# A decoder layer's first microseconds: all of x's copies on VectorE, both variances moved up, long constant products between the turns

## The chip, the cores and the metric

The kernel runs on one core of one Trainium2 chip. The metric is the device time of one execution in microseconds (us); the figure before is the median of three runs.

## The reference, cut to what matters

One decoder layer over 512 tokens with 16 learned meta tokens ahead of them (528 in all), model width 1024, all in float32:

```python
def rmsnorm(x, g):
    y = x32 * lax.rsqrt(jnp.mean(x32 * x32, axis=-1, keepdims=True) + EPS)
    return y * g

def swiglu(h, w_gate, w_up, w_down):
    return (jax.nn.silu(h @ w_gate) * (h @ w_up)) @ w_down

h = concatenate([meta, x])                                    # 528 x 1024
h = h + 0.5 * swiglu(rmsnorm(h, ffn1_norm), ffn1_w_gate, ffn1_w_up, ffn1_w_down)
h = h + token_mixing(rmsnorm(h, mix_norm), ...)               # linear and sparse attention
h = h + 0.5 * swiglu(rmsnorm(h, ffn2_norm), ...)
return rmsnorm(h, final_norm)[:, N_META:]
```

Only the first two lines of the layer matter here: how x gets into the kernel's layout, its first norm, and the first products of the first feed-forward part (FFN). The hidden width of that part is 2816.

## The kernel before

The kernel is one program per engine, each in an order written out by hand, with semaphores between them. The activations are kept turned: `h` is 128 features (partitions) by 8 feature tiles by 528 tokens. float32 products of weights are made of three products of two-part operands: a high part (`xh`, `wh`) and a rest (`xl`, `wl`). ScalarE makes the high parts of weights (`hi(u)` for unit u) and of x (`high_x`), GpSimd makes the rests of weights (`lo(u)`), VectorE the rests of x.

**The start**, which is what the change touches. SyncE issues the loads of x in four tiles of 128 tokens, then of the first four weight units; ScalarE's queue issues the 16 meta tokens and the vectors (gains, biases). Then:

- TensorE first runs ten products of the constants `ones` and `ident`, 128 columns each, into a bank that nobody reads (L2511). Then it turns x: ten *turns* n = 0 to 9, each four transposes of 128x128 (two turns per token tile; turns 0 and 1 are the meta tokens, 16 wide), turn n into PSUM bank n mod 8 (L2540), with one transpose of the vectors ahead of turn 4 (L2531).
- Each turn is copied from PSUM to `h` by `keep_x` (L448 to L456): turns 0 to 8 on VectorE (L456), turn 9 on ScalarE (L454).
- ScalarE squares and sums each 128-token tile of x straight from the loaded rows (L2049), VectorE that of the meta tokens (L2317). `x_variance(0)` (L2310, L2312; VectorE, after the copy of turn 5) is for the meta tokens and tiles 1 and 2, `x_variance(1)` (after the copy of turn 7) for tiles 3 and 4. `x_roots` (L2040, ScalarE) takes the root of each; the first one stands in ScalarE's order between the squares of tile 3 and of tile 4.
- The roots are put on diagonals: tiles 0 to 2 by GpSimd (L1835), tiles 3 and 4 by ScalarE (L2056). TensorE's `spread(0)` and `spread(1)` (L2522) multiply `ones` with them, which puts each token's factor on all partitions (PSUM banks 6 and 7). `spread(0)` waits for eight copies (`x_kept` 8).
- VectorE waits for all copies and for the spread, then makes `xn` = h times gain times factor, one of eight feature tiles at a time (L2336), then the eight rests `xl` (L2341), which need ScalarE's `xh` (L1912).
- ScalarE: diagonals, copy of turn 9, `hi(0)` (L1885), four `xh`, `hi(1)`, four `xh`, and on to `hi(2)`.
- TensorE's `first_products` (L2406) is six groups of 16 matmuls, 264 columns each: `wh`(unit 0) with `xh`, `wl`(0) with `xh`, `wh`(1) with `xh`, `wl`(1) with `xh`, then `wh`(0) and `wh`(1) with `xl`. Only the first group waits for each `xh`, and the fifth for each `xl`. After them comes the next unit's product (L2371), and from there to the end of the kernel TensorE is fed almost without a pause.

Of the kernel before, what the change touches and what calls it, by code (L numbers as in the profile page):

```python
# [26 lines left out]
ACT = mybir.ActivationFunctionType  # L27
AX_X = mybir.AxisListType.X

P = 128  # L30
# [179 lines left out]
def build(nc, x, meta, ffn1, ffn2, mix_norm, w_in, w_a2, b_a, head_norm, w_out, final_norm,  # L210
          cos_t, sin_t, out):
    ctx = ExitStack()
    with ctx:  # L213
        def sb(name, shape, dt=F32, scope=ctx):
            return scope.enter_context(nc.sbuf_tensor(name, shape, dt))

        def sem(name):
            return ctx.enter_context(nc.semaphore(name))

        ps = ctx.enter_context(nc.psum_tensor("ps", [P, 8, 512], F32))  # L220
# [14 lines left out]
        ident = sb("ident", [P, P])  # L235
        ones = sb("ones", [P, P])
# [140 lines left out]
        x_turned, x_kept = sem("x_turned"), sem("x_kept")  # L377
# [64 lines left out]
        def x_cols(n):  # L442


            t = n // 2
            return (META + (t - 1) * P, P) if t else (0, META)

        def keep_x(eng, n):  # L448
            c, w = x_cols(n)
            eng.wait_ge(x_turned, n + 1)  # L450
            src = ps[:, n % 8, 0:4 * w].rearrange("p (k n) -> p k n", k=4)
            dst = h[:, 4 * (n % 2):4 * (n % 2) + 4, c:c + w]
            if n == 9:
                eng.activation(dst, src, ACT.Copy).then_inc(x_kept_act, 1)  # L454
            else:
                eng.tensor_copy(dst, src).then_inc(x_kept, 1)  # L456

        x_kept_act, x_squared = sem("x_kept_act"), sem("x_squared")

        x_inv, x_root, x_spread = sem("x_inv"), sem("x_root"), sem("x_spread")  # L460
        x_diag, x_diag_pool = sem("x_diag"), sem("x_diag_pool")
# [4 lines left out]
        def x_pieces(t):  # L466

            c, w = x_cols(2 * t)
            return [(a, max(c, a * HALF) - a * HALF, slice(max(c, a * HALF) - c, min(c + w, (a + 1) * HALF) - c))
                    for a in range(2) if max(c, a * HALF) < min(c + w, (a + 1) * HALF)]  # L470
# [65 lines left out]
        def pe_mixer(pe, product, product_k, norm_product):  # L536
# [166 lines left out]
            def tails(e):  # L703

                b, _, s, w = att_step(0)
                if e == 0:
                    pe.wait_ge(v_kept, 6)
                else:
                    pe.wait_ge(tail_done, 1)
                for hd in range(e, HEADS, 2):  # L710
                    rows = slice(HD * e, HD * (e + 1))
                    mm = pe.matmul(ps[0:w, TAIL_BANK, tail_cols(hd)], pjb[rows, hd // 2, s:s + w],
                                   pjb[rows, 4 + hd // 2, 512:TOK], start=True, stop=True)
                mm.then_inc(tail_done, 1)
# [312 lines left out]
        def act_mixer(act, hi, prep_hi, root):  # L1027
            def keep_part(bank, dst, u, parts):
                ((_, t, n),) = parts
                act.wait_ge(w_used, Q_USED[u])  # L1030
                act.activation(dst[:, t:t + n], ps[:, bank, 0:n], ACT.Copy).then_inc(pj_kept, 1)
# [607 lines left out]
        def _(sp):  # L1639
# [24 lines left out]
            def ffn_loads(weights, u0, number):  # L1664
                _, w_gate, w_up, w_down = weights
                gate_v = w_gate.rearrange("(k p) f -> p k f", p=P)
                up_v = w_up.rearrange("(k p) f -> p k f", p=P)
                down_v = w_down.rearrange("(k p) d -> p k d", p=P)
                for f in range(PLAIN):
                    for e, v in enumerate((gate_v, up_v)):  # L1670
                        load(u0 + 2 * f + e, v[:, :, f * P:(f + 1) * P], cols())

                def load_down(g, d):
                    f0, cnt = GROUPS[g]
                    load(U_DOWN[number, g, d], down_v[:, f0:f0 + cnt, d * P:(d + 1) * P],
                         lambda s: s[:, 0:cnt * P].rearrange("p (k n) -> p k n", k=cnt))

                for d in range(PRE_DOWN):
                    load_down(0, d)
                for g, (f0, cnt) in enumerate(GROUPS):  # L1680
                    for m in range(cnt if g else 0):
                        for e in range(2):
                            f = f0 + 2 * (m // 2) + e
                            load(U_PAIR[number, g, m] + e, (up_v if m % 2 else gate_v)[:, :, f * P:(f + 1) * P], cols())
                        for e in range(2):
                            load_down(*step_down_of(g, m, e))
                for d in range(KT):
                    load_down(len(GROUPS) - 1, d)
# [188 lines left out]
        def _(act):  # L1877
            def hi(u):
                slot, n, c = u % RING, WIDTH[u], -(-WIDTH[u] // HALF_UNIT)
                if u == U_MIX + M_IKW:  # L1880
                    act.wait_ge(ikw_loaded, 16)
                act.wait_ge(w_in_slot[slot], 16 * (u // RING + 1))
                if Q_FREE[u]:
                    act.wait_ge(w_used, Q_FREE[u])
                act.activation(places(0, PLACE[u], c)[:, 0:n], raw[:, slot, 0:n], ACT.Copy).then_inc(w_hi, c)  # L1885
# [168 lines left out]
            act.wait_ge(x_root, 2)  # L2054
            for t in range(3, 5):
                act.activation(diag[:, t, :], ident[:, :], ACT.Copy, scale=xvar[:, t:t + 1]).then_inc(x_diag, 1)  # L2056
            keep_x(act, 9)
            hi(0)
            for d in range(KT):
                high_x(d)  # L2060
# [13 lines left out]
        def _(dve):  # L2074
# [233 lines left out]
            def x_variance(i):  # L2308
                dve.wait_ge(x_squared, X_PARTS[i].stop - 1)
                dve.tensor_scalar(xvar[:, X_PARTS[i]], xsum[:, X_PARTS[i]], 1.0 / D, EPS, ALU.mult, ALU.add).then_inc(x_inv, 1)  # L2310
                dve.wait_ge(x_inv, 2 * i + 2)
                dve.reciprocal(xvar[:, X_PARTS[i]], xvar[:, X_PARTS[i]]).then_inc(x_inv, 1)  # L2312
# [3 lines left out]
            meta_squares = t01[0:META, :, :].rearrange("p f n -> p (f n)")[:, 0:D]  # L2316
            dve.tensor_tensor_reduce(out=meta_squares, in0=xin[0:META, 0, :], in1=xin[0:META, 0, :], scale=1.0, scalar=0.0,  # L2317
                                     op0=ALU.mult, op1=ALU.add, accum_out=xsum[0:META, 0:1]).then_inc(x_inv, 1)
            for n in range(9):
                if n == 4:  # L2320
                    dve.wait_ge(vecs_turned, 1)
                    dve.tensor_copy(vecs[:, :], ps[:, 7, 0:4 * KT + 3]).then_inc(vecs_kept, 1)
                keep_x(dve, n)
                if n == 5:
                    dve.wait_ge(x_inv, 1)
                    x_variance(0)
                if n == 7:
                    x_variance(1)
            dve.wait_ge(x_kept, 9)
            dve.wait_ge(x_kept_act, 1)  # L2330
            dve.sem_inc(h_done, KT)
            dve.wait_ge(vecs_kept, 1)
            dve.wait_ge(x_spread, 5)
# [23 lines left out]
        def _(pe):  # L2357
# [149 lines left out]

            pe.wait_ge(consts, 2)

            for n in range(10):  # L2510
                pe.matmul(ps[:, 6, 0:P], ones[:, :], ident[:, :], start=True, stop=True)  # L2511

            def spread(i):

                for t in range(X_PARTS[i].start, X_PARTS[i].stop):
                    if i == 0:
                        pe.wait_ge(x_diag_pool, t + 1)
                    else:
                        pe.wait_ge(x_diag, t - X_PARTS[1].start + 1)
                    n = P if t else META  # L2520
                    for bank, c, cols in x_pieces(t):
                        mm = pe.matmul(ps[:, 6 + bank, c:c + cols.stop - cols.start], ones[0:n, :], diag[0:n, t, cols],  # L2522
                                       start=True, stop=True)
                    mm.then_inc(x_spread, 1)

            for n in range(10):
                t, half = n // 2, n % 2
                w = x_cols(n)[1]
                if n == 4:
                    pe.wait_ge(const_loaded, 96)  # L2530
                    pe.transpose(ps[:, 7, 0:4 * KT + 3], vec_rows[:, :],  # L2531
                                 ident[0:4 * KT + 3, 0:4 * KT + 3]).then_inc(vecs_turned, 1)
                if n == 7:
                    pe.wait_ge(vecs_kept, 1)
                pe.wait_ge(x_loaded[t], 16)
                if n >= 8:
                    pe.wait_ge(x_kept, n - 7)
                for k in range(4):
                    c = (4 * half + k) * P
                    mm = pe.transpose(ps[:, n % 8, k * w:(k + 1) * w], xin[0:w, t, c:c + P], ident[0:w, 0:w])  # L2540
                mm.then_inc(x_turned, 1)

            pe.wait_ge(x_kept, 8)
            spread(0)
            spread(1)
            ffn(U_FFN1, 0, 0)
            pe_mixer(pe, product, product_k, norm_product)
            ffn(U_FFN2, 1, 2)
# [2 lines left out]
            for n in range(8):  # L2551
                half, t = divmod(n, 4)
                tokens = slice(META + t * P, META + (t + 1) * P)
                if n == 4:
                    pe.wait_ge(ss_done, 4 * KT)
                    for c in range(4):
                        mm = pe.matmul(ps[:, 7, c:c + 1], ss[:, META + c * P:META + (c + 1) * P], ones[:, 0:1],  # L2557
                                       start=True, stop=True)
# [45 lines left out]
```

## Time and profile before

| | |
|---|---|
| median of three runs | 1070.98 us (1069.23 to 1072.9) |
| the profiled execution: its own time | 1073.09 us |
| its span | 1071.4 us |
| TensorE matmul busy | 1047.1 us (98%) |
| VectorE, ScalarE, GpSimd busy | 781.4, 464.2, 659.0 us |
| mean granted TensorE clock | 0.993 |

The profile is one execution. Its time and span differ by 1.7 us, which lies outside the instructions. In rows of the timeline the first figure is the start and the second the time from the first start to the last end of the merged instructions. PE is TensorE, DVE VectorE, ACT ScalarE, POOL GpSimd. The granted clock is recorded as a share of 2.4 GHz; ahead of its first recorded event, at 11 us, it is shown as 1.00, and there the durations must be read instead.

### The profile page before, as it was taken

What the parts mean: (1) busy time and instruction counts of PE and PEld (TensorE: products, weight loads), DVE (VectorE), ACT (ScalarE), POOL (GpSimd) and SP (SyncE); (2) the same over time, 40 slices, a digit from 0 to 9 for tenths busy, and PEclk for the clock granted to TensorE, in tenths of its full rate; (3) what the DMA queues carried; (4) which work ended last, traced back from release to release, by engine and by line L of the source; (5) the groups of instructions that cost most, each with busy time, mean ns of one, the idle gap of its engine ahead of it and who ended that gap; (6) DMA issues with size and microseconds to landing.
All of it is one profiled execution on the core that took longest, in us unless ns stands there. A gap on an engine that the chain in (4) does not pass through costs nothing. (4 is left out here: it accounts for less than half of the span.)

```text
span 1071.4 us, 19526 instructions
## 1 busy us (share of the span) xinstructions
PE 1047.1 (98%) x7427; PEld 946.1 (88%) x7427; DVE 781.4 (73%) x1251; ACT 464.2 (43%) x732; POOL 659.0 (62%) x747
## 2 busy tenths in 40 slices
PE   8999999999999999999999999999899999999997
PEld 7999999999999997788767678778799999999986
DVE  6647897677675587699575596478879977877835
ACT  6424444334343354552355526453434443443425
POOL 4948677787686277089721303356767877777840
PEclk8999999999999999999999999999999999999999
DMA  6233243323332344344321101222233434333321
GB/s 198 85 96 94 78 113 112 110 83 105 108 106 75 107 117 111 81 117 117 85 58 40 41 21 60 79 67 81 72 98 99 118 109 112 87 108 109 89 59 79
DMA packets 172256, 98.69 MB, mean 92 GB/s; under 512 B 6787, under 2 KB 167606, under 8 KB 172166
## 3 DMA queue, kind: packets, MB, share of 16 engines
q1 hardware_dynamic: 172064, 97.38, 32.3%
q8 instruction: 59, 0.97, 0.4%
q14 instruction: 31, 0.25, 0.1%
q10 hardware_dynamic: 102, 0.08, 0.0%
HBM read 91.18 MB, written 2.10 MB: 87 GB/s over the span
## 5 line engine op out<-in xcount | busy, mean ns | idle before, releaser
L1776 POOL TENSOR_TENSOR wl<-raw,wh 128x256 fp32r<-128x256 f32 x292 | 250.4, 892 | 212.6 <-ACT wh L1885 173.2
L1776 POOL TENSOR_TENSOR wxl<-raw,wxh 128x256 fp32r<-128x256 f32 x240 | 230.3, 985 | 151.6 <-ACT wxh L1885 151.2
L2371 PE MATMUL ps<-ah,wxh 128*128 128x264 f32 (+1 forms) x456 | 122.4, 323 | 2.8 <-DVE h L2175 2.4
L2371 PE MATMUL ps<-ah,wxl 128*128 128x264 f32 (+1 forms) x456 | 122.2, 322 | 0.0
L2371 PE MATMUL ps<-al,wxh 128*128 128x264 f32 (+1 forms) x456 | 122.0, 322 | 0.0
L2175 DVE SCALAR_TENSOR_TENSOR h<-ps,h 128x528 f32<-128x528 f32 (+1 forms) x96 | 66.5, 693 | 70.1 <-PE ps L2371 70.1
L2371 PE MATMUL ps<-xh,wh 128*128 128x264 f32 (+3 forms) x336 | 102.6, 348 | 2.3 <-DVE h L2175 1.1
L2490 PE MATMUL ps<-xh,wh 128*128 128x264 f32 (+1 forms) x360 | 102.1, 284 | 0.9 <-DVE h L2175 0.9
L2490 PE MATMUL ps<-xl,wh 128*128 128x264 f32 (+1 forms) x360 | 102.0, 283 | 0.0
L2490 PE MATMUL ps<-xh,wl 128*128 128x264 f32 (+1 forms) x360 | 101.6, 282 | 0.0
L2371 PE MATMUL ps<-xl,wh 128*128 128x264 f32 (+3 forms) x336 | 97.4, 332 | 0.0
L2371 PE MATMUL ps<-xh,wl 128*128 128x264 f32 (+3 forms) x336 | 97.2, 332 | 0.0
L1885 ACT ACTIVATE wxh<-raw 128x512 fp32r<-128x512 f32 (+2 forms) x88 | 53.3, 607 | 76.4 <-PE ps L2371 76.4
L2371 PEld LDWEIGHTS ps<-ah,wxh 128*128 128x128 f32 x456 | 75.7, 188 | 8.6 <-POOL wxl L1776 2.5
L2371 PEld LDWEIGHTS ps<-ah,wxl 128*128 128x128 f32 x456 | 75.9, 189 | 6.8
L2371 PEld LDWEIGHTS ps<-al,wxh 128*128 128x128 f32 x456 | 76.0, 189 | 5.2
L1776 POOL TENSOR_TENSOR wl<-ws,wh 128x256 fp32r<-128x256 f32 x72 | 69.0, 990 | 9.4 <-ACT wh L1903 9.4
L2371 PEld LDWEIGHTS ps<-xh,wh 128*128 128x128 f32 (+1 forms) x336 | 57.2, 187 | 18.7 <-issue 9.4
L1926 ACT ACTIVATE ah<-ubuf 128x528 fp32r<-128x528 f32 (+1 forms) x36 | 23.0, 640 | 110.7 <-DVE ubuf L2278 99.9
L2490 PEld LDWEIGHTS ps<-xh,wh 128*128 128x128 f32 x360 | 68.1, 189 | 1.6 <-DVE wl L2138 1.1
L2490 PEld LDWEIGHTS ps<-xl,wh 128*128 128x128 f32 x360 | 67.9, 189 | 0.5
L2490 PEld LDWEIGHTS ps<-xh,wl 128*128 128x128 f32 x360 | 68.0, 189 | 0.0
(319 smaller groups left out, 2975.0 us busy)
## 6 DMA issues: line engine op xcount, KB each, us to landing
raw<-in_ffn_w_gate SPq DMA_DIRECT2D x44, 512.0 KB, 4.1
raw<-in_ffn_w_up SPq DMA_DIRECT2D x44, 512.0 KB, 4.7
raw<-in_ffn_w_down SPq DMA_DIRECT2D x80, 256.0 KB, 2.8
raw<-in_w_in SPq DMA_DIRECT2D x28, 512.0 KB, 4.1
raw<-in_w_out SPq DMA_DIRECT2D x8, 512.0 KB, 3.4
xin<-in_x SPq DMA_DIRECT2D x4, 512.0 KB, 5.8
raw<-in_ffn_w_down SPq DMA_DIRECT2D x16, 128.0 KB, 2.2
out<-xin SPq DMA_DIRECT2D x4, 512.0 KB, 3.6
```

Of the source, the lines that this page charges most:

```text
L1776: op = pool.tensor_tensor(dst[:, part], src[:, part], high[:, part].bitcast(F32), ALU.subtract)
L1885: act.activation(places(0, PLACE[u], c)[:, 0:n], raw[:, slot, 0:n], ACT.Copy).then_inc(w_hi, c)
L1926: act.activation(ah[:, j, tk], src, ACT.Copy).then_inc(a_hi, 1)
L2175: dve.scalar_tensor_tensor(out=as_parts(h[:, d, tk], norm), in0=psum_parts(bank, norm), scalar=0.5, in1=as_parts(h[:, d, tk], norm), op0=A ...
L2371: mm = pe.matmul(ps[0:m, bank + a, 0:width], places(lo, PLACE[u], -(-WIDTH[u] // HALF_UNIT))[:, k * P:k * P + m], r[:, tile, t:t + width], ...
L2490: mm = pe.matmul(ps[:, seven_bank(v, i), 0:w], places(lo, at_p[wn], 1)[:, k * P:(k + 1) * P], x_operand(xlo, xn_, w, number)[:, k, :], sta ...
```

## The change

- `keep_x` of turn 9 moves from ScalarE to VectorE; its own semaphore `x_kept_act` goes, and VectorE waits for ten `x_kept`.
- `x_variance(0)` moves from after the copy of turn 5 to after that of turn 3, `x_variance(1)` from after turn 7's to after turn 6's.
- On TensorE the ten constant products of 128 columns become two of 512 columns, into bank 3. One more of these follows each of turns 5, 7 and 9, and one follows `spread(1)`. The one after turn 5 waits for the copy of turn 3, since it overwrites bank 3.

```diff
         def keep_x(eng, n):
...
-            if n == 9:
-                eng.activation(dst, src, ACT.Copy).then_inc(x_kept_act, 1)
-            else:
-                eng.tensor_copy(dst, src).then_inc(x_kept, 1)
+            eng.tensor_copy(dst, src).then_inc(x_kept, 1)
...
                 act.activation(diag[:, t, :], ident[:, :], ACT.Copy, scale=xvar[:, t:t + 1]).then_inc(x_diag, 1)
-            keep_x(act, 9)
             hi(0)
...
-            for n in range(9):
+            for n in range(10):
                 if n == 4:
                     dve.wait_ge(vecs_turned, 1)
                     dve.tensor_copy(vecs[:, :], ps[:, 7, 0:4 * KT + 3]).then_inc(vecs_kept, 1)
                 keep_x(dve, n)
-                if n == 5:
+                if n == 3:
                     dve.wait_ge(x_inv, 1)
                     x_variance(0)
-                if n == 7:
+                if n == 6:
                     x_variance(1)
-            dve.wait_ge(x_kept, 9)
-            dve.wait_ge(x_kept_act, 1)
+            dve.wait_ge(x_kept, 10)
...
-            for n in range(10):
-                pe.matmul(ps[:, 6, 0:P], ones[:, :], ident[:, :], start=True, stop=True)
+            def keep_warm(times):
+
+                for _ in range(times):
+                    pe.matmul(ps[:, 3, :], ones[:, :], ones[:, :].unsqueeze(1).broadcast_to([P, 4, P]), start=True, stop=True)
+
+            keep_warm(2)
...
                 mm.then_inc(x_turned, 1)
+                if n == 5:
+                    pe.wait_ge(x_kept, 4)
+                if n in (5, 7, 9):
+                    keep_warm(1)
 
             pe.wait_ge(x_kept, 8)
             spread(0)
             spread(1)
+            keep_warm(1)
             ffn(U_FFN1, 0, 0)
```

## Rows read from the trace of the kernel before

**Rows 1.** The page: busy us, share of the span and instructions of each engine.
```profile
PE 1047.1 (98%) x7427; PEld 946.1 (88%) x7427; DVE 781.4 (73%) x1251; ACT 464.2 (43%) x732; POOL 659.0 (62%) x747
```
**Rows 2.** Timeline of TensorE, 1 to 34 us: start, us, engine, line, operation, count.
```profile
1.59 4.63 PE L2511 MATMUL ps<-ident,ones 128*128 128x128 f32 x20 [1.59 <-POOL ident L1765]
6.15 2.93 PE L2540 MATMUL ps<-ident,xin 16*128 16x16 f32 x16
...
9.26 3.66 PE L2540 MATMUL ps<-ident,xin 128*128 128x128 f32 x24
13.42 2.01 PE L2522 MATMUL ps<-diag,ones 16*128 16x16 f32 x12 [0.50 <-DVE h L456]
14.65 0.78 PE L2522 MATMUL ps<-diag,ones 128*128 128x128 f32 x4
17.17 2.74 PE L2406 MATMUL ps<-xh,wh 128*128 128x264 f32 x8 [1.74 <-ACT xh L1912]
...
22.79 2.93 PE L2406 MATMUL ps<-xh,wl 128*128 128x264 f32 x16
25.56 2.10 PE L2406 MATMUL ps<-xh,wh 128*128 128x264 f32 x16
...
33.30 0.40 PE L2371 MATMUL ps<-xh,wh 128*128 128x264 f32 x2
```
**Rows 3.** Timeline of VectorE in the same stretch.
```profile
9.12 0.69 DVE L456 COPY h<-ps 128x512 f32<-128x512 f32 x1 [0.16 <-PE ps L2540]
...
11.82 0.16 DVE L2310 TENSOR_SCALAR xvar<-xsum 128x3 f32<-128x3 f32 x1
...
12.10 1.26 DVE L456 COPY h<-ps 128x512 f32<-128x512 f32 x2
...
15.59 5.49 DVE L2336 SCALAR_TENSOR_TENSOR xn<-h,vecs,ps 128x528 f32<-128x528 f32 x8 [1.08 <-PE ps L2522]
21.00 9.19 DVE L2341 TENSOR_TENSOR xl<-xn,xh 128x528 fp32r<-128x528 f32 x8
```
**Rows 4.** Timeline of ScalarE in the same stretch.
```profile
12.33 1.04 ACT L2049 ACTIVATE ubuf<-xin 128x1024 f32<-128x1024 f32 x1
...
14.19 0.70 ACT L2056 ACTIVATE diag<-ident,xvar 128x128 f32<-128x128 f32 x2
14.79 0.57 ACT L454 ACTIVATE h<-ps 128x512 f32<-128x512 f32 x1
15.27 1.04 ACT L1885 ACTIVATE wh<-raw 128x1024 fp32r<-128x1024 f32 x1
16.39 2.67 ACT L1912 ACTIVATE xh<-xn 128x528 fp32r<-128x528 f32 x4
```
**Rows 5.** Tile xin: when its loads were issued, and how long they took to land.
```profile
L1657 SPq DMA_DIRECT2D xin<-in_x x4: 379/426/433, 0.8 to 2.2; - x4
...
DMA to landing us min/median/max: 3.6/5.3/7.0
```
**Rows 6.** Timeline of TensorE, one float32 product of 512 columns at the full clock.
```profile
711.17 1.02 PE L2380 MATMUL ps<-ss,ones 128*128 128x512 f32 x2
```
**Rows 7.** The turns alone (L2540), by stretch: us, busy and count, clock, DMA share, GB/s.
```profile
9.26:10.98 1.72, 1.72 (x8) 1.00 1.20 290
10.98:12.70 1.72, 1.72 (x18) 1.00 1.20 290
```
**Rows 8.** All of TensorE by stretch, same columns, around falls and rises of the clock.
```profile
635.56:638.97 3.41, 1.52 (x10) 1.00 0.00 0
...
14.40:17.80 3.40, 1.47 (x10) 1.00 0.37 91
17.80:21.20 3.40, 2.73 (x9) 0.50 0.15 42
21.20:24.60 3.40, 3.40 (x16) 0.50 0.39 117
24.60:28.00 3.40, 3.40 (x30) 1.00 0.52 154
```

More of the change, by code:

```diff
@@ L452, in keep_x @@
             dst = h[:, 4 * (n % 2):4 * (n % 2) + 4, c:c + w]
-            if n == 9:
-                eng.activation(dst, src, ACT.Copy).then_inc(x_kept_act, 1)
-            else:
-                eng.tensor_copy(dst, src).then_inc(x_kept, 1)
-        x_kept_act, x_squared = sem("x_kept_act"), sem("x_squared")
+            eng.tensor_copy(dst, src).then_inc(x_kept, 1)
+        x_squared = sem("x_squared")
         x_inv, x_root, x_spread = sem("x_inv"), sem("x_root"), sem("x_spread")
```

## The prediction

> **What bounds the kernel now.** I read the page first: TensorE is busy for 98% of the span, the others for 43 to 73% [rows 1]. So a microsecond that TensorE gains or loses in front of the steady part should arrive at the end nearly whole, and one gained anywhere else only if TensorE waited for it. The change touches nothing behind L2406, so I read the timeline of TensorE from its first instruction to the first matmul of the next unit, at 33.30 [rows 2]. That start, 33.30, is the number to forecast: the edit is worth what it moves it. Then I put the other engines' timelines beside it [rows 3, 4].
>
> Four things are to be seen. (a) TensorE pauses after the turns, then for 1.7 us between the spread's end at 15.43 and the first product at 17.17, and shortly for each `xh` of the first group. (b) `xn` starts at 15.59, right behind the spread's end (14.65 + 0.78). It paces `xh`, and `xh` the first group. (c) VectorE runs without a gap from 15.59 to the last `xl` at 30.19 (21.00 + 9.19) [rows 3]. The fifth group's last two matmuls need that last `xl`, and a group of 16 follows: 18 x 0.121 us (groups three and four are 16 matmuls each from 25.56 on, 0.121 apart) = 2.2 us, so VectorE alone would allow 32.5. (d) TensorE is behind that by 0.8 us, and the clock is why: the granted clock is 0.50 (1.2 GHz) from 17.8 to 24.6 [rows 8], the second group takes 2.93 us where the third takes 2.10 [rows 2], and from the first group's end at about 22.6 to 24.6 the low clock costs half of 2.0 us, 1.0 us. 22.6 + 80 x 0.121 + 1.0 = 33.3, which is what is recorded. So at most 0.8 us is there to be won by the clock alone, unless `xn` also starts sooner.
>
> **The change, part by part.**
>
> *The warm-up products.* Ten products of 128 columns run from 1.59 to the first turn at 6.15 [rows 2]. That is 1280 columns in 4.56 us, 3.56 ns a column, so 1.82 us for 512 at that clock and 0.91 at twice it. A float32 product of 512 columns at the full clock is recorded with 1.02 us [rows 6]. Both hold the latency of a last record, so I take a little less, 1.7 low and 0.85 high; 0.1 more on each product would add 0.2 to 0.3 us to the sum. Two low ones end at 5.0. So turn 0 can start at 5.1 instead of 6.15: 1.1 us sooner, and turns 0 to 5 with it, all still at the low clock. Their last now ends near 9.9 (before, 9.26 + 1.74 = 11.0).
>
> *The rate of the turns.* Eight transposes fit between 9.26 and 10.98, eighteen between 10.98 and 12.70 [rows 7]: 0.215 us each, then 0.10. The clock rose at 11.0, though the record shows 1.00 before. A turn is 0.86 us low and 0.41 high. I place the rise at the same 11.0.
>
> *Constant products between the turns.* One of 512 columns after turns 5, 7 and 9: 0.85 us each high, 1.7 low. They stand in TensorE's queue ahead of the next turns, of `spread(0)` and so of `xn`; nothing hides them but the copies that VectorE still has to make. The first starts at 9.9 low, reaches 11.0 with 64% done, ends at 11.3. Its added wait, for the copy of turn 3, costs nothing: that copy ended at 9.81 (9.12 + 0.69 [rows 3]) and now at 8.7. Turns 6 and 7: 12.1. Second product: 13.0. Turns 8 and 9: 13.8. Third: 14.7.
>
> *Copies and variances.* Variance 0 costs VectorE 0.28 us (11.82 to 12.10) and now runs near 8.8, when the squares of tiles 1 and 2 are long done. ScalarE's fourth square waited for its root until 12.33 [rows 4]; now it waits for the root at about 9.3, or for tile 4 itself, which landed by 2.2 + 7.0 = 9.2 at the latest [rows 5]. It ends near 10.7 instead of 13.5: 2.8 us sooner. Variance 1, which had to wait for that square, moves to behind copy 6. Copy 6 runs 11.9 to 12.5, variance 1 to 12.9, copy 7 to 13.5, copy 8 to 14.2, copy 9 (0.63 us, half of the row at 12.10, to 0.69 on VectorE, against 0.57 on ScalarE [rows 4]) to 14.9. The diagonals of tiles 3 and 4 are ready at 14.0 instead of 14.9.
>
> So all that `spread` waits for is ready before 14.7, and TensorE's own queue is late now: the third constant product. The twelve records of both spreads took from 13.42 to about 14.4 and from 14.65 to 15.43 [rows 2], 1.6 us without the wait. 14.7 + 1.6 = 16.3, and `xn` starts at 16.4: 0.8 us later than before. **That is the middle of my sum**; by the same steps it is 15.7 if the clock is already high at 9.9 (first product 0.85) and 18.2 if it rises only at 14.4.
>
> *ScalarE without copy 9.* `hi(0)` starts at 14.0 instead of 15.27 [rows 4] and ends before `xn`'s first tile. Before, it ended at 16.31, 0.08 us ahead of the first `xh`, so it was no bound; its earlier end gives nothing but an earlier `lo(0)`, which is hidden too.
>
> *The product after `spread(1)`.* 0.85 us in a gap of 1.7 us: it ends at 17.2, the first `xh` is ready at 17.8. At the low clock, 1.7 us, it would end at 18.0 and cost 0.2.
>
> *The end of the sum.* VectorE's bound moves with `xn`: 32.5 + 0.8 = 33.3. TensorE's own: first group's end 22.6 + 0.8 = 23.4, less 0.2 if the clock is high, + 9.7 = 32.9 to 33.1, plus what the low clock costs. If it never falls, 33.3, change 0.0. If it falls in the first group and rises at 24.6 as before, half of 1.3 is lost: 33.7, change +0.4.
>
> *Does the clock fall again?* The fall at 17.8, and another behind 639, came after stretches in which TensorE was busy for 1.47 us of 3.40 and 1.52 of 3.41 [rows 8]. In the first group two matmuls, 0.40 us together at the full clock, follow each `xh`, and these come 0.67 us apart (2.67 for four [rows 4]) with `hi(1)`'s 1.04 us in the middle: a share of 0.6 at best, 0.4 with the hole. Filling one pause of 1.7 us ahead of it does not fill those. I think a fall likelier than not.
>
> One page speaks against this kernel's rows. First the rows: between 6.15 and 10.98 TensorE did only transposes, and their rate doubled at 10.98. The Trainium skill (TensorE: Matmul & The Clock Gate, Part 4: PE-mode transpose) says that transposes don't engage the full clock. By that rule the turns would have stayed slow and the constant products would be needed; it would give the second rival below. The trace speaks against it.
>
> **The rivals.**
>
> *A: a trade within the measurement* (my forecast). Turns start 1.1 us sooner, three products cost 2.6 to 3.0 us, `xn` is 0.1 to 1.2 us later, and the clock gives back 0 to 1. Change +0.3: 0.0 and +0.4, weighted to the fall.
>
> *B: slower.* The clock stays low through the turns (with the moved start TensorE works at a different place when it would rise), to 14.4. `xn` at 18.2: +2.7. From there VectorE's bound gives 35.2, and TensorE's own 22.6 + 2.7 + 9.7 = 35.0, plus up to 2.4 us if a fall comes late and lasts over groups two to four (low for 4.8 us): 37.4. Change +1.9 to +4.1. It decides if the four turns behind 9.9 go at 0.215 us a transpose. For it: nothing but turns and products filled the stretch ahead of 10.98, and the mix changes. Against it: long products fill TensorE at least as well as ten short ones.
>
> *C: faster.* The clock is high before 9.9 and holds throughout: `xn` at 15.7, VectorE's bound 32.6, change -0.7. To gain over 3.2 us, `xn` would have to start before 12.5, when x's seventh copy is not done. So only something outside this stretch could show that.
>
> *D: the change doesn't do what it says*: the clock falls and rises where it did. That is the upper half of A.
>
> **How the numbers follow.** About 0.3% (3.2 us) is what a measurement of this kernel can tell from no change. A has 0.72, C 0.13, B 0.15, of which half is over 3.2 us. The profiled execution took 1073.09 us (span 1071.4 and 1.7 around), 2.1 above the median of 1070.98; the difference of +0.3 worked out on it is added to the median: 1071.3. The runs before spread by 1.8 us down and 1.9 up, more than the whole of A. So the range is -0.7 and +1.9 widened by most of that: 1068.7 to 1074.0. Faster 0.04, same 0.88, slower 0.08.
>
> **What would show each step.** Turn 0 at 5.1; fourth square at 9.4; turns 6 to 9 at 0.10 us a transpose; third constant product's end at 14.7, and `xn` waiting for L2522 at 16.4; the first product at 17.9; a clock of 0.50 somewhere between 18 and 25; `xl`'s end at 31.0; the next unit (33.30 before) between 33.0 and 34.0. It is wrong if `xn` starts before 15.5, if TensorE's pauses in the first group vanish, or if the time moves by what happens behind 34 us.

## The result and the profile after

The changed kernel takes 1074.47 us (median of 12 runs, 1072.46 to 1076.86) against 1070.22 for the kernel before beside it (12 runs, 1068.98 to 1073.6). The ratio is 1.0035, 95% interval 1.0023 to 1.0046: slower by 2.5 to 4.9 us. The forecast was 1071.3 in a range of 1068.7 to 1074.0 at the old level. The median lies 0.5 us above that range; as a ratio on the old median (1070.98 x 1.0035 = 1074.7, interval 1073.4 to 1075.9) its lower end touches it. "Within 0.3%" had 0.88, and the middle of the measurement is on the other side of that bound, in rival B. One execution of the experiment l below took 1697.01 us at a mean granted clock of 0.555 and stands in no ratio or mean here.

The profiled execution of the changed kernel took 1076.35 us, its span is 1074.6, 3.2 more than before's 1071.4. TensorE in its timeline (start, us, line, operation, count), to be read against [rows 2]:

```profile
1.58 3.78 PE L2508 MATMUL ps<-ones 128*128 128x512 f32 x4 [1.58 <-POOL ident L1762]
5.30 2.93 PE L2539 MATMUL ps<-ident,xin 16*128 16x16 f32 x16
...
8.40 1.97 PE L2539 MATMUL ps<-ident,xin 128*128 128x128 f32 x8
10.17 1.36 PE L2508 MATMUL ps<-ones 128*128 128x512 f32 x2
11.37 1.04 PE L2539 MATMUL ps<-ident,xin 128*128 128x128 f32 x8
12.24 1.02 PE L2508 MATMUL ps<-ones 128*128 128x512 f32 x2
13.10 1.04 PE L2539 MATMUL ps<-ident,xin 128*128 128x128 f32 x8
13.98 1.02 PE L2508 MATMUL ps<-ones 128*128 128x512 f32 x2
14.93 1.70 PE L2521 MATMUL ps<-diag,ones 16*128 16x16 f32 x12
16.47 1.02 PE L2508 MATMUL ps<-ones 128*128 128x512 f32 x2
18.34 1.10 PE L2401 MATMUL ps<-xh,wh 128*128 128x264 f32 x4 [0.85 <-ACT xh L1909]
...
23.96 3.72 PE L2401 MATMUL ps<-xh,wl 128*128 128x264 f32 x16
27.48 2.29 PE L2401 MATMUL ps<-xh,wh 128*128 128x264 f32 x16
...
35.41 0.40 PE L2366 MATMUL ps<-xh,wh 128*128 128x264 f32 x2
```

Between 8.40 and 16.5 TensorE has no pause, and yet it is behind: three of its products serve nothing. The next unit starts at 35.41 instead of 33.30, 2.1 us later. VectorE and ScalarE (their timelines, against [rows 3, 4]):

```profile
8.87 0.16 DVE L2306 TENSOR_SCALAR xvar<-xsum 128x3 f32<-128x3 f32 x1
...
13.74 1.29 DVE L453 COPY h<-ps 128x512 f32<-128x512 f32 x2 [0.18 <-PE ps L2539]
16.76 5.49 DVE L2331 SCALAR_TENSOR_TENSOR xn<-h,vecs,ps 128x528 f32<-128x528 f32 x8 [1.73 <-PE ps L2521]
22.17 9.19 DVE L2336 TENSOR_TENSOR xl<-xn,xh 128x528 fp32r<-128x528 f32 x8
```
```profile
9.38 1.04 ACT L2046 ACTIVATE ubuf<-xin 128x1024 f32<-128x1024 f32 x1
...
13.85 1.04 ACT L1882 ACTIVATE wh<-raw 128x1024 fp32r<-128x1024 f32 x1
17.56 2.67 ACT L1909 ACTIVATE xh<-xn 128x528 fp32r<-128x528 f32 x4 [2.67 <-DVE xn L2331]
```

The moves did what they say: the fourth square starts at 9.38 instead of 12.33, the copies end at 15.03. But VectorE then stands idle for 1.73 us and waits for L2521, the spread, which waits behind the constant products. The clock, as TensorE's busy time, count and granted clock by stretch, against [rows 8]:

```profile
17.80:21.00 3.20, 2.01 (x8) 1.00 0.56 161
21.10:24.60 3.50, 2.84 (x11) 0.50 0.02 5
24.60:27.90 3.30, 3.30 (x17) 0.50 0.46 137
27.90:31.30 3.40, 3.40 (x31) 1.00 0.17 42
638.90:642.40 3.50, 2.71 (x6) 0.50 0.00 0
642.40:645.70 3.30, 3.30 (x13) 0.50 0.00 0
```

It is low (1.2 GHz) from 21.1 to 27.9, where before it was low from 17.8 to 24.6. That is the same 6.8 us, but they lie elsewhere. Before, about 5 us of them fell on the first group, which waits for `xh` anyway; now about 3 us do, and the rest covers the second group and the start of the third, which wait for nothing. The second group takes 3.72 us instead of 2.93, the third 2.29 instead of 2.10. The remaining 1.1 us of the 3.2 (3.2 - 2.1) lie outside the stretch that the change touches: behind 639 the clock was low for 6.8 us in this execution and for 3.4 in the one of before. Whether the change has a part in that is not shown.

### The profile page after: what moved, and what is told of

It reads as the page before. It is cut to its first block and busy times, and to the rows that moved or that the text cites. A ratio compares the mean times of both kernels' runs of the same rounds, so it can differ in the third digit from the quotient of the medians.

```text
span 1074.6 us, 19510 instructions
## 1 busy us (share of the span) xinstructions
PE 1051.3 (98%) x7419; PEld 945.3 (88%) x7419; DVE 780.2 (73%) x1252; ACT 463.9 (43%) x731; POOL 655.9 (61%) x747
## 5 line engine op out<-in xcount | busy, mean ns | idle before, releaser
L1773 POOL TENSOR_TENSOR wxl<-raw,wxh 128x256 fp32r<-128x256 f32 x240 | 227.4, 973 | 155.8 <-ACT wxh L1882 155.4
```

What stands on the lines that cost most here:

```text
L1773: op = pool.tensor_tensor(dst[:, part], src[:, part], high[:, part].bitcast(F32), ALU.subtract)
```

## The experiments

All were measured in 12 runs (b in 10, l in 11), each beside 33 to 35 runs of the kernel before, in three series of four kernels. "Means" is the difference of the mean times within a series. Executions of one and the same kernel spread by 5 to 6 us, in groups: those of before lie near 1069, 1071.5 and 1073 to 1074, and in the three series every one below 1070 us has a mean granted clock of 0.995 or 0.996, every one above it 0.993 or less. The first 12 had half of theirs near 1069 (mean 1070.7), the 103 of the three series 19 (means 1071.9, 1072.5, 1071.8). Against all 115 (mean 1071.9) the changed kernel (mean 1074.9) is slower by 3.0 us; the ratio of 1.0035 has some luck of the first 12 in it.

**First series: which products cost?** My theory then was that the product behind the spread puts the clock's fall off and so moves the low clock onto the groups that wait for nothing. The numbers of `xn` and of the next unit are each from one profiled execution.

*a_no_between*, the changed kernel without the products between the turns:

```diff
                 mm.then_inc(x_turned, 1)
-                if n == 5:
-                    pe.wait_ge(x_kept, 4)
-                if n in (5, 7, 9):
-                    keep_warm(1)
```

> The changed kernel without the three constant products between the turns; the one behind the spread stays. My theory (the products behind the spread put the clock's fall off, so that the low clock lies on the second and third group instead of the first): xn starts near 14.5 (1.1 sooner than before), yet the clock falls near 21 and is low to about 28; the next unit starts near 34.4, time 1.1 us above before. Rival (the late xn alone costs, the fall comes when it comes): same clock as in the kernel without either product, time 1 us below before.

Measured: ratio 0.9993 (0.9979 to 1.0006), means -1.0 us. `xn` at 14.62 and the next unit at 32.94. The clock fell at 18.2 and not near 21, although the product behind the spread stood in its place. That is the rival's case.

*b_no_tail*, the changed kernel without the one behind the spread:

```diff
             spread(1)
-            keep_warm(1)
```

> The changed kernel without the constant product behind the spread; the three between the turns stay. My theory: xn at 16.8 as in the changed kernel, TensorE pauses 1.7 us or more before the first product, the clock falls near 17.7 and is back near 24.5, next unit near 33.8; time 1.6 us below the changed kernel, 0.5 above before. Rival (only xn's delay counts): as the changed kernel, 2 to 3.7 us above before.

Measured: ratio 1.0028 (1.0017 to 1.0038), means +3.0 us. `xn` at 17.31, next unit at 34.81. That is the rival's case again.

*c_neither*, with both edits:

> The changed kernel with neither the three products between the turns nor the one behind the spread: the moves on VectorE and ScalarE and the two long products at the start. Both theories: xn near 14.5, next unit 32.0 to 32.7, time 0.6 to 1.3 us below before. If it is not below before, the moves themselves cost something that I don't see.

Measured: ratio 0.9996 (0.9983 to 1.0010), means -0.2 us. `xn` at 13.78, next unit at 31.53 in the profiled execution. Both are sooner than expected, but a gain of 0.6 us or more is not shown: the interval holds it and also no change.

*d_before_tail*, the kernel before and that one product:

```diff
...
             spread(1)
+            keep_warm(1)
```

> The kernel before with one constant product of 512 columns behind the spread, nothing else. My theory: xn stays at 15.6, the clock falls near 21 instead of 17.8 and rises near 28 instead of 24.6, next unit near 34.9, time 1.6 us above before. Rival (the fall isn't moved by this product, or a filled pause can only help): 0 to 0.8 us below before.

Measured: ratio 0.9986 (0.9974 to 0.9999), means -1.5 us.

My theory fell: the product behind the spread costs nothing that shows (3.0 us over before with it, and 3.0 without it in b), and d is, if anything, faster than before. What the changed kernel loses goes with the three between the turns: +3.0 against -1.0 in a, and +3.0 in b against -0.2 in c. Both steps are above the 2.6 us that the three products take at the full clock, the second within its interval (3.2, about 2.0 to 4.4). The profile of d also shows something I had not seen in the one profile of before. Up to the spread it is the same program, but its turns are quick from the start and `xn` starts at 13.96 instead of 15.59 (TensorE, VectorE, then the clock by stretch):

```profile
6.14 1.71 PE L2545 MATMUL ps<-ident,xin 16*128 16x16 f32 x16
8.30 2.84 PE L2545 MATMUL ps<-ident,xin 128*128 128x128 f32 x24
```
```profile
13.96 4.14 DVE L2336 SCALAR_TENSOR_TENSOR xn<-h,vecs,ps 128x528 f32<-128x528 f32 x6 [1.08 <-PE ps L2527]
```
```profile
14.60:19.80 5.20, 2.88 (x13) 1.00 0.36 92
19.90:23.30 3.40, 3.38 (x15) 0.50 0.27 78
23.30:26.70 3.40, 3.40 (x30) 1.00 0.52 153
```

24 transposes in 2.84 us where [rows 2] have 3.66: the clock rose at 6.2, right behind the warm-up products (4.63 us in both executions), and not at 11. The low stretch lasted 3.4 us and not 6.8. So the same instructions have executions with `xn` at 14.0 and others at 15.6, and the page I forecast from was of the slower kind, 1073.09 us against a median of 1070.98.

The start is not all of it. The span of d is 4.2 us shorter than that of before (1067.2 against 1071.4), and its next unit, at 31.83, only 1.5 sooner. The other 2.7 us lie far behind the change, where the clock was low twice for 3.4 us in before and not at all in d (TensorE by stretch, before, then d):

```profile
638.97:642.39 3.42, 3.42 (x14) 0.51 0.00 0
772.08:775.50 3.42, 3.42 (x11) 0.51 0.06 20
```
```profile
637.00:642.00 5.00, 5.00 (x46) 1.00 0.00 0
768.00:774.00 6.00, 5.83 (x37) 1.00 0.17 51
```

In the fourteen profiles what follows the next unit's start takes 1035.4 to 1035.5 us where the clock is low in none of it but the last 10 us (d, i, j, l), 1036.8 to 1036.9 with one more stretch of 3.4 (a, k), 1037.5 to 1038.1 with two, and 1039.1 to 1039.2 with one of 6.8 and one of 3.4 (the changed kernel, e, p). These stretches alone spread the time by as much as the change moves it.

**Second series: single parts on the kernel before.**

*e_products_only*, all of TensorE's products, the moves undone (`keep_x` of turn 9 on ScalarE, the variances behind turns 5 and 7):

> The changed kernel with the copy of turn 9 back on ScalarE and both variances back in their old places, so TensorE's constant products alone. Theory now (the three products between the turns are paid in full in front of xn, 2.5 us at the full clock and up to 3.5 with the low one; everything else is small): 0 to 1 us above the changed kernel, 3.5 to 5 above before. Rival (the moves on VectorE cost part of it): below the changed kernel by 1 us or more.

Measured: ratio 1.0028 (1.0012 to 1.0044), means +2.6 us. That is below the 3.5 to 5 us that I expected. Against the changed kernel's +3.0 the moves change nothing that shows.

*i_moves_only*, the moves alone, with the ten products of 128 columns and no others:

> The moves on VectorE and ScalarE alone, with before's ten constant products ahead of the turns and none elsewhere. Theory: the fourth square runs near 9.4 and xn starts at 13.6 to 14.5, 0.2 us sooner than before where the clock rises early (near 6) and 1.1 sooner where it rises late (near 11); time 0.3 to 1 us below before. Rival (one copy more on VectorE in front of xn eats the gain or more): 0 to 0.7 above.

Measured: ratio 0.9994 (0.9980 to 1.0009), means -1.2 us; `xn` at 13.79 in an execution whose clock rose early.

*j_short_warm*, the kernel before with the shorter warm-up:

```diff
...
-            for n in range(10):
-                pe.matmul(ps[:, 6, 0:P], ones[:, :], ident[:, :], start=True, stop=True)
...
+            keep_warm(2)
```

> The kernel before with two constant products of 512 columns in place of the ten of 128 ahead of the turns, nothing else. Theory: turns start 0.9 us sooner, but the vectors' transpose must wait for their load until 8.1, so at most 0.9 us is won where the clock rises late and nothing where it rises early: -0.9 to 0 us. Rival (3.4 us of products instead of 4.6 let the clock rise later, or fall again at once, in more of the executions): +0.5 to +1 us.

Measured: ratio 1.0001 (0.9986 to 1.0016), means -0.5 us. No verdict between the two theories: the half microsecond is within the interval.

*k_between_only*, the kernel before with the edit of a put in:

> The kernel before with the three constant products after turns 5, 7 and 9, nothing else. Theory: they are paid in full, xn starts 2.5 to 3.4 us later than in the kernel before at the same rise of the clock; time +2.5 to +3.4 us, most of what the whole change costs (+3.7). Rival (the products hide beside VectorE's copies and the loss comes from several parts): +1 or less.

Measured: ratio 1.0005 (0.9991 to 1.0020), means +0.5 us. A miss: I expected 2.5 us at least. In the profile the three products run at the full clock and `xn` starts at 17.05, against 15.59 at a similar rise (10.5 against 11.0):

```profile
12.29 1.29 DVE L456 COPY h<-ps 128x512 f32<-128x512 f32 x2 [0.30 <-PE ps L2545]
...
17.05 2.11 DVE L2336 SCALAR_TENSOR_TENSOR xn<-h,vecs,ps 128x528 f32<-128x528 f32 x3 [2.33 <-PE ps L2527]
```

That is 1.5 us later, for 2.6 us of products: with before's order TensorE paused ahead of the spread (0.50 us) and within it (from about 14.4 to 14.65) [rows 2], since the fourth square and the copies were late, and those pauses (0.75 us) and the clock's rise, which came 0.4 us sooner, are about the 1.1 us that don't show. By this reading the moves take the pauses away and so lay the products bare. The next unit of this execution starts at 35.48, 2.2 us later than in the profile of before, while the means differ by 0.5: what the three products cost here on average, one profile doesn't say.

The series has one more comparison. e is k with the shorter warm-up and the product behind the spread, and by the means it is 2.1 us slower (interval about 0.9 to 3.4). Each of the two alone costs nothing that shows (j, d). So most of what e loses comes only when the products between the turns meet one of them. b, as slow without the product behind the spread, speaks for the warm-up.

**Third series: warm-up, length, and the sum of the good parts.**

*m_after_ten*, the whole change with before's ten products ahead of the turns (the edit of j backwards):

> The whole change except that the ten products of 128 columns stand ahead of the turns again, in place of the two of 512. Theory now (the short warm-up and the products between the turns make it slow together: 3.4 us of products let the clock rise and lose it again, or not rise, and the products between the turns then go at the low clock in front of xn): 0 to 1 us above before, 2 to 3 us below the changed kernel. Rival (the products between the turns cost their length whatever is ahead of them): 2.5 us or more above before.

Measured: ratio 1.0015 (1.0002 to 1.0029), means +1.9 us: between the theory's 0 to 1 and the rival's 2.5 or more.

*l_between_128*, the whole change with short products between the turns:

```diff
                 if n in (5, 7, 9):
-                    keep_warm(1)
+                    pe.matmul(ps[:, 3, 0:P], ones[:, :], ones[:, :], start=True, stop=True)
```

> The whole change with 128 columns instead of 512 in the three products between the turns. If their length is what costs: a quarter of the price remains, xn near 15, time at most 0.8 us above before, 2.5 us below the changed kernel. If it is not (the order, the wait for the copy of turn 3, the switch of operands): as the changed kernel.

Measured: ratio 0.9990 (0.9980 to 1.0001), means -0.6 us. The wait and the order are the changed kernel's; only 384 of each 512 columns are gone, and with them 3.6 us by the means, against 1.9 us that they take at the full clock (3 x 384/512 x 0.86). So the length is what costs, but more than itself. In the two profiled executions `xn` is 2.0 us sooner, the next unit (32.61) 2.8, since the low stretch lasts 3.4 us and not 6.8, and what follows it is 3.7 us shorter, since l has no low stretch there. `xn` is at 14.77, with the clock's rise at 10.5, near the changed kernel's 10.8 and 16.76:

```profile
10.40 0.42 PE L2544 MATMUL ps<-ones 128*128 128x128 f32 x2
10.65 1.04 PE L2539 MATMUL ps<-ident,xin 128*128 128x128 f32 x8
11.52 0.39 PE L2544 MATMUL ps<-ones 128*128 128x128 f32 x2
```

*o_moves_tail*, the moves and the product behind the spread:

> The parts of the change that showed no cost: the moves on VectorE and ScalarE and the product behind the spread, with before's ten products ahead of the turns and none between them. The sum of the two single results is 1.2 + 1.5 us by the means: 1 to 2.7 us below before. If both win the same time, 1 to 1.5.

Measured: ratio 0.9993 (0.9978 to 1.0008), means -0.9 us. It differs from m in the edit of a alone, and in both profiles the clock rose early. `xn` starts at 13.52 here and at 15.55 there, the next unit at 31.30 and 34.31; by the means the three products cost 2.7 us (1073.6 against 1070.9, interval about 1.3 to 4.1), about their length of 3 x 0.86. The gain itself, 0.9 us, is just short of what I expected and not told from nothing. The two gains of i and d don't add up here; that they win the same time is likely, but not shown.

*p_moves_tail_fill*, that kernel with constant products in the first group, where TensorE waits:

```diff
                                            stop=(k == KT - 1 and r is xl))
+                        if v == u and r is xh and not lo and k < KT - 1:
+                            for _ in range(4 if k == KT // 2 - 1 else 1):
+                                pe.matmul(ps[:, 5, 0:P], ones[:, :], ident[:, :], start=True, stop=True)
```

> As the kernel with the moves and the product behind the spread, and with one constant product of 128 columns (four after the fourth) behind each pair of matmuls of the first group, where TensorE waits for xh. Theory: the clock doesn't fall in the first group, the groups behind it run at 0.121 us a matmul, and VectorE's last xl sets the next unit's start, near 31: 0.5 to 1.5 us below the kernel without them. Rival: the fillers stand in front of the next pair, or the clock falls anyway and they go at the low clock: 0.5 us or more above it.

Measured: ratio 0.9980 (0.9970 to 0.9990), means -1.6 us: faster than both kernels, 1.1 to 3.2 us below before by the ratio. Over o alone it is 0.7 us by the means, as expected in size, but less than these runs can tell; the profile is what speaks for the fillers. The fillers fit between the pairs, the clock stays at 1.00, and the second group takes 2.10 us:

```profile
17.32 0.51 PE L2401 MATMUL ps<-xh,wh 128*128 128x264 f32 x2
17.67 0.38 PE L2406 MATMUL ps<-ident,ones 128*128 128x128 f32 x2
17.99 0.51 PE L2401 MATMUL ps<-xh,wh 128*128 128x264 f32 x2
...
22.10 2.10 PE L2401 MATMUL ps<-xh,wl 128*128 128x264 f32 x16
```
```profile
16.70:20.20 3.50, 3.39 (x23) 1.00 0.40 116
20.20:23.60 3.40, 3.40 (x27) 1.00 0.14 40
23.60:27.00 3.40, 3.40 (x30) 1.00 0.53 154
```

`xn` started at 15.14 in this execution, whose clock rose late (10.8), and the next unit at 32.11: 1.2 us sooner than in the profile of before for an `xn` that is 0.45 sooner. From `xn` to the next unit it took 17.0 us, where before took 17.7. The 0.7 us between them are nearly all of the 0.8 that the prediction put on the clock, and VectorE's bound (32.5 - 15.6 = 16.9) is what is left. In the thirteen other profiles that distance is 17.5 to 18.8 us.

## Why the prediction was right or wrong

**The bound and its reach: held.** The next unit's start moved by 2.1 us and the span by 3.2, of which 1.1 is a longer low stretch at 639. "If the time moves by what happens behind 34 us" stood among the signs of being wrong, and for a third of this pair's difference that is so.

**Warm-up and turns: held.** Turn 0 at 5.30 (forecast 5.1), since even the two low products take 3.7 us to the next start and not 3.5. Rates of 0.22 and 0.11 us a transpose; rise at 10.8 (11.0).

**Constant products between the turns: right in mechanism, slightly too small.** They were to delay `xn`, with nothing over them; `xn` at 16.4, measured 16.76. The turns behind 9.9 began 0.3 late; each product costs 0.86 high (12.24 to 13.10).

**Copies, variances, `hi(0)`: held.** Fourth square at 9.38 (9.4), last copy's end 15.03 (14.9), `hi(0)` at 13.85 (14.0). They bought nothing here, as written, because TensorE's queue was later; i has them alone, 1.2 us below before by the means, not told from nothing by its interval.

**The product behind the spread: held** for itself: no cost shows (b against the changed kernel).

**The end of the sum: this step failed.** I let the clock fall in the first group "and rise at 24.6 as before", which made +0.4. It fell at 21.1, was low for the same 6.8 us and rose at 27.9, and the groups behind the first then paid for 3.9 us at half speed where I had 1.3. That is 1.3 us more, and with `xn` 0.4 later than forecast it is the whole of the step from +0.4 to the measured +2.1; the late fall over groups two to four stood under B with "up to 2.4". The error was to take the moment of the rise from the old trace as a date, when in this stretch of every profile it came 3.4 or 6.8 us after the fall, if the clock fell at all.

**The base: mis-sized too.** I worked against one execution whose clock rose late, and knew that it was 2.1 us above the median, but took the difference as spread around the same mechanism. Where the clock rises early, before has `xn` near 14.0 (d), and m, with all the products between the turns and behind the spread, has it at 15.55, +1.6. Rival C's early rise did not come in the profile of the changed kernel (10.8). It came in others (5.8 in c), and C left out that the old kernel has it too. Against d's execution, with its next unit at 31.83, the changed kernel's 35.41 is 3.6 us later; against the one I had, 2.1. The forecast should have carried both bases. And the range ended 3.0 us above the median, where B began at +1.9 and went to +4.1: half of B lay outside it.

**The rivals.** B's size (+1.9 to +4.1) is what came; its condition, turns at the low clock up to 14.4, did not (the turns behind 10.8 took 0.11 us a transpose). Its other half, the late fall, did. D, that the clock falls and rises where it did, holds in part: it falls again and for as long, but 3.3 us later, and that is what cost. C fell.

**The page.** The prediction set a rule against this kernel's rows, and a_no_between has the plainest case for it. Its clock rose at 4.5, fell at 7.9, and rose again at 11.3, when for 3 us TensorE had run transposes alone (TensorE's timeline, then by stretch):

```profile
8.08 0.32 PE L2530 MATMUL ps<-ident,vec_rows 35*128 35x35 f32 x1 [1.46 <-DMA vec_rows<-in_gla_head_norm]
8.33 4.29 PE L2539 MATMUL ps<-ident,xin 128*128 128x128 f32 x24
```

```profile
4.60:7.90 3.30, 2.02 (x17) 1.00 1.03 403
7.90:11.30 3.40, 3.22 (x15) 0.50 1.15 307
11.30:12.50 1.20, 1.20 (x12) 0.99 1.20 289
```

The Trainium skill (TensorE: Matmul & The Clock Gate, Part 4: PE-mode transpose) says that the full clock doesn't engage for transposes. The trace disagrees for these float32 ones: no product between them was needed to raise the clock.

**What stays open.** Why the products between the turns cost so different an amount: 3.9 us (the changed kernel against a) and 3.2 (b against c) with the shorter warm-up, 2.7 (m against o) and 0.5 (k against before) with before's ten products. In a and b the clock rose about when the short warm-up ended (4.5 and 5.4) and fell again at 7.9 and 8.8, in b just before the first constant product, which then took 1.92 us. That is a mechanism by which the two parts harm each other. In the seven profiles with the short warm-up the clock rose before 7 in three and held in one of them (c); in the seven with the ten products it rose before 7 in four and held in all four (d, i, m, o). But the profiles of the changed kernel and of e show no such second fall, and how often it happens over many executions was not measured. Nor is it shown that p's gain is the same in its early-rise executions.

## What to carry to other kernels

A constant product keeps TensorE's clock up for free only where TensorE would wait anyway: in the pauses of the first group it held the clock, and together with the moves and the product behind the spread the kernel came out 1.6 us below before by the means. Ahead of work that others wait for, three of them, 2.6 us long, cost 2.7 us where nothing else differed (o and m), 3.2 with the shorter warm-up (b and c), and 0.5 us where the old order still had pauses (k). Before such a product is put in a queue, ask which engine waits for what stands behind it, and ask it again when another edit removes the pause it hid in. And where a kernel's executions fall in groups, one profile is one group: compare it with another profile of the same program before forecasting a microsecond.

## What the runs showed of the hardware

- The granted clock's first rise comes at different moments in executions of the same instructions: at 6.2 in d, at 11.0 in the profile of before, with the same ten products ahead. With the same instructions up to there, `xn` starts 1.6 us apart.
- In the fourteen profiles each stretch of low clock ahead of the kernel's last 10 us lasted 3.4 or 6.8 us. By half of the overlap, an estimate, one of 6.8 costs up to 3.4 us on dense matmuls. In the profile of before some 5 of the 6.8 us lay on matmuls that wait, and from `xn` to the next unit it cost 0.7 us against p, which had none; in that of the changed kernel 3.9 us lay on dense ones. So a later fall can be worse than an early one.
- Executions differ as much far behind the start. What follows the next unit's start is the same code in all fourteen kernels, and it took 1035.4 to 1039.2 us, with neither, one or both of the low stretches near 639 and 772.
- In this kernel float32 transposes take 0.215 us each at the low clock and 0.10 to 0.11 at the full one, and in a_no_between the clock rose after 3 us of nothing but transposes.
